# Input projections of a hybrid decoder step: split float32 halves in place of float32 products

## The reference, cut to what matters

```python
h = rmsnorm(xp, norm_mix[l])
a, b, c, d = layer_inputs(h, w_in[l], lbs[l], pos_p)   # p = split_proj(h @ w_in_l)
o_a = mixer_a_prompt(...)      # indexer scores, top 256 keys, attention
s_b, o_b = gla_prompt(...)     # gated recurrence, chunks of 64
o_c = combine_dilations(...)   # three dilated windows
s_d, o_d = gla_prompt(...)     # retention
mix = concatenate([o_a, hgrn_out(o_b), o_c, retention_out(o_d)])
xp = residual_block(xp, mix, w_out[l], norm_ffn[l], w_gate[l], w_up[l], w_down[l])
# f_b = lbf + (1 - lbf) * sigmoid(p['b_f']),  q_b = silu(p['b_q'])
```

## Time and profile before

| | |
|---|---|
| Median of three runs | 3419.17 us (3413.51 to 3424.32) |
| The profiled execution | 3413.46 us |
| Its span (first to last instruction) | 3411.8 us |
| Mean granted TensorE clock | 0.974 |
| PE busy | 3267.9 us (96%) |
| DVE busy | 1827.1 us (54%) |
| ACT busy | 516.0 us (15%) |
| POOL busy | 328.0 us (10%) |

### The profile page before, as it was taken

The page is one execution under the profiler, slowest core; times in us unless marked ns, Lnnn a source line. Parts: engine busy times, 40 slices in busy tenths (PEclk is TensorE's granted clock), DMA queues, the critical chain, the costliest instruction groups (busy, mean ns, idle before and its releaser), DMA issues.

```text
span 3411.8 us, 54621 instructions
## 1 busy us (share of the span) xinstructions
PE 3267.9 (96%) x21232; PEld 2812.9 (82%) x21248; DVE 1827.1 (54%) x3381; ACT 516.0 (15%) x1015; POOL 328.0 (10%) x594
## 2 busy tenths in 40 slices
PE   7999999898999999999989999998989999999997
PEld 4569567776899999999965685767678999999997
DVE  3599953768453333333427999256875433333335
ACT  2200112244110000000111001131432000000001
POOL 4000241000000000000040004300010000000000
PEclk9999999889999999999999999996999999999999
DMA  7211344132111111111142114432321111111112
GB/s 268 59 44 38 107 149 170 75 119 97 44 38 46 43 47 53 40 48 50 37 151 62 37 32 151 152 117 75 119 103 38 50 44 44 45 45 48 50 44 95
DMA packets 119600, 261.93 MB, mean 77 GB/s; under 512 B 18805, under 2 KB 74118, under 8 KB 116662
## 3 DMA queue, kind: packets, MB, share of 16 engines
q0 software_dynamic: 40288, 129.06, 11.9%
q1 hardware_dynamic: 74530, 114.47, 9.8%
q10 hardware_dynamic: 4516, 14.76, 1.2%
HBM read 227.10 MB, written 35.60 MB: 77 GB/s over the span
## 4 chain that ended last, share of the span: by engine, by line
PE 89%; DVE 6%; issue 2%; ACT 2%; DVEq 1%; DMA 0%; ACTq 0%; SPq 0%; POOL 0%; POOLq 0%
PE PS L1173 14%; PE PS L1171 14%; PE PS L1169 14%; PE PS L709 14%; PE PS L838 5%; PE PS L715 5%; PE PS L1060 2%; PE PS L844 2%; PE PS L1195 2%; PE PS L1197 2%; PE PS L1196 2%; PE PS L731 1%; PE PS L770 1%; PE PS L809 1%; PE PS L790 1%
## 5 line engine op out<-in xcount | busy, mean ns | idle before, releaser
L1851 DVE TENSOR_SCALAR_CACHE_REDUCE U<-U,smu 128x384 bf16<-128x384 f32 (+6 forms) x448 | 484.3, 1145 | 6.2
L709 PE MATMUL PS<-Hn,WS 128*128 128x352 f32 x1536 | 461.5, 463 | 14.7 <-DVE Hn L1774 14.7
L709 PEld LDWEIGHTS PS<-Hn,WS 128*128 128x128 f32 x1536 | 294.3, 192 | 180.6 <-issue 21.1
L2248 DVE TENSOR_TENSOR U<-PS,U 128x352 f32<-128x352 f32 x132 | 69.1, 523 | 538.3 <-ACT U L1634 538.3
L454 POOL DMA_DIRECT2D WS<-wjobs x226 | 121.6, 538 | 2396.9 <-PE PS L1173 1467.4
L1173 PE MATMUL PS<-HNHR,WSR 128*128 128x352 f32 x1920 | 346.3, 322 | 0.0
L1169 PE MATMUL PS<-HNHR,WHR 128*128 128x352 f32 x1920 | 345.3, 321 | 0.0
L1171 PE MATMUL PS<-HnR,WHR 128*128 128x352 f32 x1920 | 345.3, 321 | 0.0
L1173 PEld LDWEIGHTS PS<-HNHR,WSR 128*128 128x128 f32 x1920 | 314.5, 188 | 0.0
L1171 PEld LDWEIGHTS PS<-HnR,WHR 128*128 128x128 f32 x1920 | 313.6, 188 | 0.0
L1169 PEld LDWEIGHTS PS<-HNHR,WHR 128*128 128x128 f32 x1920 | 313.5, 188 | 0.0
(11 more groups left out here) (286 smaller groups left out, 4334.4 us busy)
## 6 DMA issues: line engine op xcount, KB each, us to landing
WS<-wjobs POOLq DMA_DIRECT2D x163, 512.0 KB, 3.9
WS<-wjobs POOLq DMA_DIRECT2D x48, 384.0 KB, 3.3
Hn<-ckT SPq DMA_DIRECT2D x16, 896.0 KB, 7.8
U<-kT_pool SPq DMA_DIRECT2D x160, 64.0 KB, 1.9
xres<-U SPq DMA_DIRECT2D x2, 4224.0 KB, 15.2
U<-xres SPq DMA_DIRECT2D x4, 2112.0 KB, 8.1
U<-v_pool SPq DMA_DIRECT2D x128, 64.0 KB, 2.1
U<-v_pool POOLq DMA_DIRECT2D x128, 64.0 KB, 2.5
```

The lines of the kernel that those rows point to most:

```text
L709: i = mm(PS[:, base + c, 0:CW], w[:, k, :], Hn[:, k, c * CW:(c + 1) * CW], start=k == 0, stop=k == KR - 1)
L1851: ts(flags[0:m, flag_at[i]:flag_at[i] + s.shape[1]], s, CANDF[0:m, i:i + 1], None, ALU.is_ge, ALU.add, accum_out=CNT[0:m, i:i + 1])
L2248: tt(out=x, in0=PS[:, 2 * (t % 3) + 1, 0:CW], in1=U[:, SIL + (t % 3) * CW:SIL + (t % 3 + 1) * CW], op=ALU.mult)
```

## The change

**What it does.** 25 of the 29 jobs (all but the first four) are computed as `split_step` in three products of float32r halves. The x half `XHR` is copied by ACT from the normalised rows, the remainder `HnR` is subtracted by POOL (`low_rows`). For each step, ACT copies the high half of the weights (`high_part`, into three places in `HNHR`), POOL subtracts the low half (`low_weights`, in place of the weights, `WSR`), two steps ahead. N jobs go in pairs: one matmul has 256 moving columns (two jobs side by side). The last token tile is a full 128 tokens. There are 22 steps: A 3 T, B 6 T, B's values (N pair), C 4 T, C's values (N pair), D 6 T, D's values (N pair); in this order, C before its values. PSUM banks 5 to 7 take the units in turn, and 0 to 4 stay with sample attention.

Results of B, C and D go through four staging places (`STAGE`) to HBM (`btok`, `ctok`, `dtok`, `bval`, `cval`, `dval`) and are read back by SP later: B's rows and values and C's after the last step, around `attend(0)`. silu and sigmoid of B are applied where ACT moves the result out of PSUM. `decay_b` moves into `attend(0)`, behind its step 12. C's 32 sample columns are kept apart (`crs`).

The sample scores of A are now spread over C's steps, one sequence at a time, and D's steps follow without them. The values of A stand behind D's last step but one unit.

```diff
-J_A, J_B, J_CV, J_C, J_D, J_OUT, J_GU = 0, 7, 15, 17, 21, 29, 37
+J_A, J_B, J_C, J_CV, J_D, J_OUT, J_GU = 0, 7, 15, 19, 21, 29, 37
-KB = [WKEY, MIX, 14848]
+KB = [BI, MIX, BI + 2048]
+        for r in range(6):
+            STEPS_P.append(("T", (J_D + r,), ((0, 1, 2, 1, 2, 0)[r],), dtok[:, r, :], ACT.Copy, 1.0))
+        STEPS_P.append(("N", (J_D + 7, J_D + 6), (1, 2), dval, ACT.Copy, 1.0))
+        S_A, S_B, S_BI, S_C, S_CV, S_D, S_DV = 0, 3, 9, 10, 14, 15, 21
@@ POOL
+                def low_rows():
+                    pool.wait_ge(pj_ps, len(PI))
+                    pool.wait_ge(x_hi, KR)
+                    for k in range(KR):
+                        pool.tensor_tensor(out=HnR[:, k, :], in0=Hn[:, k, :], in1=XHR[:, k, :].bitcast(F32),
+                                           op=ALU.subtract).then_inc(x_lo, 1)
+                def low_weights(i):
+                    for j, a in zip(*STEPS_P[i][1:3]):
+                        pool.wait_ge(wp_hi, SPLIT_NO[j] + 1)
+                    for j, a in zip(*STEPS_P[i][1:3]):
+                        pool.tensor_tensor(out=WSR[:, j % NSLOT, 0:1024], in0=slot(j, 1024),
+                                           in1=high_weights(a).bitcast(F32), op=ALU.subtract).then_inc(wp_lo, 1)
+                for i in range(NSTEP):
+                    for j in sorted(STEPS_P[i][1]):
+                        load(j + NSLOT, job_floats(j + NSLOT), j)
+                    if i + 2 < NSTEP:
+                        low_weights(i + 2)
+                    if i == S_BI:
+                        keys(3, page_numbers(pool, 3))
+                    elif i == S_C + 1:
+                        keys(5, page_numbers(pool, 5))
+                    elif i == S_C + 3:
+                        keys(7, page_numbers(pool, 7))
+                    elif i == S_D:
+                        values(0, page_numbers(pool, 0))
+                    elif i == S_D + 4:
+                        ahead = page_numbers(pool, 3)
+                    elif i == S_D + 5:
+                        values(3, ahead)
+                        values(5, page_numbers(pool, 5))
+                        values(7, page_numbers(pool, 7))
@@ SP, after the page transfers
-                sp.wait_ge(as_v, 7)
+                sp.wait_ge(un_ps, NUNIT)
...
+                sp.dma_start(br, btok).then_inc(br_in, 16)
+                sp.wait_ge(as_v, NB)
+                kept_values(U[:, BI:BI + 2048], nbi[0:NS, 8, :], bval, bv_in)
+                sp.dma_start(cr, ctok).then_inc(cr_in, 16)
+                kept_values(U[:, CV:CV + 2048], ncv[0:NS, 8, :], cval, cv_in)
@@ PE
+            def split_step(i, units=None):
+                kind, jobs, ats, _, _, _ = STEPS_P[i]
+                pe.wait_ge(wp_lo, max(SPLIT_NO[j] for j in jobs) + 1)
+                for c in units or range(UNIT[i + 1] - UNIT[i]):
...
+                    if kind == "T":
+                        for n, (w, x) in enumerate(((hi, XHR), (hi, HnR), (lo, XHR))):
+                            for k in range(KR):
+                                m = mm(out, w[:, k * P:(k + 1) * P], x[:, k, t], ...)
                     else:
...
+                        for q in range(2 if c < 4 else 1):
+                            for n, (w, x) in enumerate(((hi, XHR), (hi, HnR), (lo, XHR))):
+                                for k in range(KR):
+                                    m = mm(out, x[:, k, t:t + P], w[:, :, k * P:(k + 1) * P], ...)
@@ PE, sample_a
+                pe.wait_ge(x_lo, KR)
+                for i in range(S_A, S_C):
+                    split_step(i)
                 scores((0, 1, 2))
-                retain(L, 0)
-                scores((3, 4))
-                retain(L, 1)
-                scores((5, 6))
-                retain(L, 2, (0, 1))
+                for i, seqs in enumerate(((3,), (4,), (5,), (6,))):
+                    split_step(S_C + i)
+                    scores(seqs)
+                split_step(S_CV)
                 scores((7,))
+                for i in range(S_D, S_DV):
+                    split_step(i)
...
                 values((0, 1, 2))
-                retain(L, 4)
+                split_step(S_DV, (4,))
                 values((3, 4))
-                retain(L, 5)
                 values((5, 6))
-                retain(L, 6)
                 values((7,))
@@ DVE, attend
+                    if k == 0 and s == 12:
+                        decay_b()
```

More of the change, by code:

```diff
@@ L116 @@
 NDV, DOWN = 20992, 29504
-STAGE = [10496, 34308, 34308 + 9 * P]
-STAGED = [0, 0, 1, 2, 1, 2, 1, 2]
+STAGE = [BI + 4096 + 1152 * i for i in range(4)]
+WH_AT = [2112, 6400, 7424]
+CRS = QZA + 256
 MIXD = MIX + 6 * TT
@@ new lines, in build, with unit_bank, high_weights @@
+        S_A, S_B, S_BI, S_C, S_CV, S_D, S_DV = 0, 3, 9, 10, 14, 15, 21
+        NSTEP = len(STEPS_P)
+        UNIT = [sum(3 if q[0] == "T" else 5 for q in STEPS_P[:i]) for i in range(NSTEP + 1)]
+        NUNIT = UNIT[NSTEP]
+        STEP_OF = {j: i for i, q in enumerate(STEPS_P) for j in q[1]}
+        SPLIT_NO = {j: n for n, j in enumerate(range(J_A + 4, J_OUT))}
+        def unit_bank(u):
+            return 5 + u % 3
+        def high_weights(a):
+            return HNHR[:, :, :].rearrange("p r t -> p (r t)")[:, WH_AT[a]:WH_AT[a] + 1024]
@@ L353, in job_bank @@
+        KEPT, SENT, sent = {}, {}, [0] * 4
+        at_ = 0
+        for i in range(S_B, NSTEP):
+            KEPT[i] = (at_,) if STEPS_P[i][0] == "T" else (at_, at_ + 1)
+            SENT[i] = tuple(sent[a] for a in KEPT[i])
+            for q, a in enumerate(KEPT[i]):
+                sent[a] += 16 * (q + 1)
+            at_ = (KEPT[i][-1] + 1) % 4
         def job_bank(n):
-            return n % 2 * 3 if n < PA[0] else 5 if n == PA[0] else (n + 1) % 2 * 3
+            return n % 2 * 3
         def ffn_place(j):
@@ L1260, in _ @@
                 pe.wait_ge(rest_in, 32)
-                for group in (PA, PB, PCV, PC):
-                    project(L, group)
                 def qa(h, o, w):
@@ L1389, in project, with high_part @@
                         copy(dst[0:NS, 8, :], PS[0:NS, base + 2, 2 * nc_:3 * nc_]).then_inc(pj_ev, 1)
-            def score():
+                    if n == 1:
+                        act.wait_ge(nrm_done, 2 * NCH)
+                        act.wait_ge(x_out, 16)
+                        for k in range(KR):
+                            copy(XHR[:, k, :], Hn[:, k, :]).then_inc(x_hi, 1)
+            def high_part(L, i):
+                for j, a in zip(*STEPS_P[i][1:3]):
+                    loaded(act, L, j)
+                    copy(high_weights(a), slot(j, 1024)).then_inc(wp_hi, 1)
@@ L1392, in score @@
+            def score(L):
                 u = 0
@@ L2282, in _ @@
                 select()
-                decay_b()
                 attend(0)
```

289 lines of the change are left out of this document (141 added, 148 removed).

## The result

The changed kernel takes 3474.4 us, the median of four runs (3471.2 to 3479.3), against 3419.7 us for the kernel before on the same chip: a ratio of 1.016, 95% interval 1.014 to 1.018. It is slower by 1.6%. The forecast was 3393 us with a range of 3352 to 3446, so the direction was wrong and the time lies outside the range. The profiled execution has a span of 3473.0 us against 3411.8: 61.2 us more, 30.6 per layer, where the sum said 13.1 less.

What follows compares the result with a forecast made beforehand. TensorE's stream was taken as the bound. Per layer, 21 us won before attention, less 5 for clock and 2.9 for `decay_b`, gave -13.1, -26.2 in all: 3387.3 from the profiled execution, 3393 us as median; range 3352 to 3446.

Steps and rivals of the forecast that it cites:

- Products: Split T and N products ahead of attention: T steps 54 us less, N pairs 21 less, gross 75 us per layer.
- The rival of a bound by weight loads: N pairs: float32r weight loads set the time, 40 ns more per matmul, +25.9 us per layer, 3445 us; chance 0.15.
- no faster products: Rival for the changed jobs: split T products no faster here than float32, 3500 us; chance 0.03.
- Scores and keys: Sample scores among C's steps: six groups, +7.4 us per layer; PE waits 7.2 us twice for keys, 14.3 us.
- The meeting with DVE: At the bias product PE meets DVE's selection, ending at 438.5 us, at the same moment as before; it does not bind.
- The tail: Sample values after D's steps: PE waits 10.3 + 11.1 + 11.1 = 32.5 us for page transfers.
- the clock term: After the tail's waits, last value group at half speed and attention starting slow: +5 us per layer, bounds 0 and 8.
- Clock and `decay_b`: Half clock after the tail's waits, +5 us; `decay_b` moved into attention, +2.9 us; both per layer.
- Rows through HBM: Rival within attention: rows read back for C's cached keys come 30 us slower, +10 per layer, 3413 us; chance 0.07.
- POOL reload: Rival: each subtraction behind a weight transfer costs POOL 8.75 us idle, +48 us per layer, 3490 us; chance 0.06.

Runs made afterwards that it cites:

- the kernel with low rows on DVE: Changed kernel with the eight low-row subtractions moved from POOL to DVE, where it waited for the samples' scores: 3412.1 us, ratio 0.999 to the kernel before.
- the one with two units ahead: Low rows on DVE, early pages and new tail order, plus D's first two value units ahead of the bias product: 3372.6 us, ratio 0.989 to before.

## Why the prediction was wrong

**The step that failed** is the one sentence that gave it no working: x's halves (POOL 8 x 2.55 us, ahead of 142) and the low weights "I cost at nothing: they lie beside PE's steps". The durations were right (2.40 us each), and they were over before PE wanted them. But I asked only whether PE would wait for them, not which other engine works in the same 19 us. It was DVE, at the head of a chain DVE, ACT, PE that has two buffers of slack. What the runs showed in place of nothing: the first split product stood 30.5 us late (172.66 instead of 142.21). The projections ahead had ended 1.4 us earlier, so the score stage took 31.9 us more in the first layer and 29.9 in the second. In both, 17.0 us are the hold: the first sum stands at 111.23 instead of 94.2 (95.66 moved by the 1.4 us that the projections ended earlier). The other 14.9 and 12.9 us are the half clock. That the hold brought it is shown for the second layer, where it fell behind PE's wait; in the first it had fallen 6 us before the wait, so there the hold may only have prolonged it. Undoing it gave 62.3 us back over both layers. The forecast with this term, 3393 + 61 = 3454, would still have been low by 20 us; those are in the terms below.

**Products.** Right. From 412.87 to 482.08 stand six T steps: 11.53 us each, 160 ns a matmul (forecast 11.45). From 383.51 to 409.26 an N pair: 25.75 us, 119 ns a matmul (forecast 25.7). The rival of a bound by weight loads is refuted, and so is that of no faster products. Over the columns' own time at 2.4 GHz (the granted clock is 1.00 there) a matmul takes some 13 ns more, at 256 columns as at 352. The Trainium skill's rule that I had weighed (TensorE: Matmul & The Clock Gate, section on LDWEIGHTS), by which a pair would be 23.6 us, comes out 2.1 us too low.

**Scores and keys.** Right in kind: a wait of 6.18 and one of 4.85 us (forecast 7.2 each) and none of note for sequence 7. I missed that a wait of this length costs again in the group behind it: 6.45 and 5.97 us instead of 3.69, at a granted clock of 0.56 in the first, together 16.1 per layer against 14.3. From the first split product to the bias it was 309.4 us against 305.5.

**The meeting with DVE** was right by luck of two errors: PE came late, and so did the selection, which started 30 us later and took 9 us longer, because its one-operand steps also wait for POOL's low weights. The rows of the timeline of the kernel after:

```profile
186.04 0.88 DVE L1930 TENSOR_SCALAR_CACHE_REDUCE U<-U,smu 128x640 bf16<-128x640 f32 x1
186.10 2.40 POOL L527 TENSOR_TENSOR WSR<-WS,HNHR 128x1024 fp32r<-128x1024 f32 x1 [0.31 <-ACT HNHR L1368]
...
209.14 2.38 POOL L527 TENSOR_TENSOR WSR<-WS,HNHR 128x1024 fp32r<-128x1024 f32 x1 [0.32 <-ACT HNHR L1368]
...
209.54 2.01 DVE L1933 TENSOR_SCALAR smu<-sm,CT 128x7 uint32<-128x7 f32 x1
```

The counting instruction with its running sum is as quick beside POOL as without (0.88 us), the comparison on 7 columns takes 2.01 us instead of 0.23. With the same waits of two-operand steps beside it (one on 32x2080 took 4.36 us instead of 2.37), in the kernel with low rows on DVE this is what makes the selection end at 450.5 instead of 438.5 and bind.

**The tail.** The three waits are there, 11.15, 10.39 and 13.74 us, 35.3 against 32.5, and the groups behind them took 5.0, 5.8 and 6.3 us instead of 3.7, at a granted clock of 0.74 around the first and 0.60 around the last. From t0 (517.1, when the values of samples 0 to 2 end) to attention it took 57.1 us against 48.3: 2.8 more of waits and 6.0 more in the three groups. Of these 6.0 I had the last group's 2.6, but in the clock term. One term of the chain was mis-sized: POOL issued the last page at 558.2 us and PE had it at 566.3, 8.1 us where I had 2.5. In these 8.1 us the DMA engines moved 384 GB/s, all of them busy; SP had issued bias tiles and cached keys (544.8 to 549.6 us). That the pages queued behind these was not tested.

**Clock and `decay_b`.** From attention to the normalisation ahead of the feed-forward part (DVE on `Hn`, 932.33 before and 962.38 now) 388.2 us against 381.7: +6.5, where I had 7.9 for both terms, the last group's 2.6 included. Right in size; the split between the two terms was not tested. Rows through HBM did not come late, and no wait for them is in the trace. Nor did POOL reload: ahead of its subtractions of the low weights it stood idle for 0.3 to 1.9 us, waiting for ACT's copy, and not for 8.75.

So the sum missed, in the first layer: by 30.5 us ahead of the first split product, 3.9 from there to the bias, 0.4 to t0 (35.1 us against 34.7), 8.8 from t0 to attention and -1.4 in attention. That is 42.2 of the 43.7 us per layer. The other 1.5 is in my own sum: the times of its steps put attention 19.5 us earlier, and I went on with 21.

## What to carry to other kernels

When work is added to an engine that looks idle, list what every other engine does in those microseconds, above all DVE for work on GpSimd: "beside PE's steps" is no cover if PE's steps depend on DVE. Look for it in a trace as a tiny DVE instruction as long as a GpSimd one beside it. And count a stall of PE with what it does to the clock behind it: two waits of 7 to 8 us came with 42 us in all. How much of such a loss is the stall's doing has to be read from each layer, since the clock also fell where nothing held PE.

Where products get faster, transfers that hid behind them become the bound. Deal out what is left as cover behind the start of the chain, not ahead of it; that and earlier page numbers won 29 us here (3412.1 to 3383.4). Two units that fill a wait for DVE won some 4 us per layer more by the profile.

## What the runs showed of the hardware

- GpSimd arithmetic on SBUF shuts out DVE's one-operand instructions between SBUF and SBUF (TENSOR_SCALAR). The one on 128x32 waited to the end of GpSimd's row of instructions in all six layers that had such a row: 18.91 us beside eight subtractions, 11.40 beside six, 5.94 beside six copies; with a drain behind the first it took 2.38. That is no rule for every case. In the changed kernel two subtractions without a gap ran from 473.74 to 480.08 us. A TENSOR_SCALAR on 32x2080 (1.23 us by itself) began at 474.54, ended at 477.83, 1.1 us behind the first of them, and the second took 3.38 us instead of 2.4. So this one got in between; what decides it was not tested. Two-operand ones (TENSOR_TENSOR) get in between, one for each GpSimd instruction: 12.40 us for six. TENSOR_SCALAR_CACHE_REDUCE is not touched: 32 of them on 32x2080 took 75.6 us in the kernel before and 75.6 beside the low weights. The Trainium skill (SBUF — State Buffer, section on the two separate sides) says that DVE in a two-port mode or with two SBUF inputs and GpSimd take a shared pair of ports as an exclusive lock, held for a whole instruction, and that the loser fully blocks. By that rule the trace agrees that they exclude each other; for how long, the traces say more: the one-operand form on 128x32 waited for the whole row.
- A wait of PE brought the scores to half clock: in the four layers that began them at full clock and then had PE waiting for a hold (2.85 to 15.2 us), the clock was at half behind the wait. The score stage can also fall to half clock without any hold. Over all profiles, it ran at half clock, at least for a part, in all 6 layers with an uninterrupted series from POOL at its head, and in 4 of 16 without one. These four began at half clock; their stages took 56.9 to 65.3 us, 8 to 15 us more than the 49.3 at full clock once GpSimd's wait of 3.5 us in the longest is taken off. In the first layer the fall goes with the time at which the scores began and not with the hold: in the four profiles where they began at 91.2 to 91.6 us the clock fell at about 94, in the eight where they began at 92.2 to 92.9 us it did not. What decides it stayed open. It may be why runs of one kernel lie 20 to 40 us apart (3358 to 3400 for the one with two units ahead). The longer runs do have the lower mean granted clock (0.963 at 3358.5 us, 0.954 at 3400.0), but in which stage it fell is known for the profiled runs alone.
- Subtraction of 128x1056 float32: 2.40 us on GpSimd, 1.18 on DVE.
